# Gating a tile of attention one iteration pair earlier, and moving the splits of y and the gate of the last group in the state-space mixer

## The reference, cut to what matters

```
def mamba2_mixer(h, w_in, ...):
    z, xbc, dt = split(h @ w_in)
    xbc = silu(causal_depthwise_conv(xbc, conv_w, conv_b))
    xs, Bm, Cm = split(xbc)
    y = ssd_chunked(xs, dt, A, Bm, Cm) + d_skip[:, None] * xs
    y = y * silu(z)
    y = rmsnorm(y, gate_norm)
    return y @ w_out

def swa_sink_mixer(h, cos, sin, w_in, sinks, w_out):
    q, k, v, gate = split(h @ w_in)
    ...
    o = einsum(p / denom, vb)
    o = o * silu(gate)
    return o @ w_out
```

## Time and profile before

| what | value |
|---|---|
| median of three executions | 1911.11 us |
| the profiled execution: its own time | 1910.12 us |
| its span, first to last instruction | 1908.2 us |
| mean granted TensorE clock | 0.986 |
| TensorE busy (products) | 1849.4 us, 97% |
| TensorE busy (weight loads) | 1473.4 us, 77% |
| VectorE busy | 1063.2 us, 56% |
| GpSimd busy | 890.2 us, 47% |
| ScalarE busy | 583.2 us, 31% |

### The profile page before, as it was taken

How to read it: one execution, slowest core, us unless ns; L and a number is a source line. 1 busy time by engine, 2 the same in 40 slices (tenths; PEclk the granted TensorE clock), 3 DMA queues, 4 the chain that set the end, 5 groups by cost and what they waited for, 6 DMA issues and landing times.

```text
span 1908.2 us, 25036 instructions
## 1 busy us (share of the span) xinstructions
PE 1849.4 (97%) x9691; PEld 1473.4 (77%) x9691; DVE 1063.2 (56%) x1660; ACT 583.2 (31%) x1035; POOL 890.2 (47%) x902
## 2 busy tenths in 40 slices
PE   7999999899999899999999999999999999999998
PEld 5788888687777577478888888887777788888887
DVE  6888887865778647453333321357778733333212
ACT  3444444512334322142111100136656521111001
POOL 4444445354533155245555555654332455555553
PEclk9999999999999899999999999999999999999999
DMA  8777776568555387848888888986653598888875
GB/s 209 166 151 158 150 160 145 130 160 179 124 123 118 72 187 167 202 97 190 194 194 194 194 182 191 203 188 133 133 127 85 125 200 194 194 191 198 181 173 134
DMA packets 217317, 309.92 MB, mean 162 GB/s; under 512 B 22864, under 2 KB 171504, under 8 KB 217200
## 3 DMA queue, kind: packets, MB, share of 16 engines
q0 software_dynamic: 42912, 148.65, 45.5%
q1 hardware_dynamic: 169872, 154.28, 25.9%
q10 hardware_dynamic: 4416, 5.39, 1.1%
HBM read 153.12 MB, written 2.10 MB: 81 GB/s over the span
## 4 chain that ended last, share of the span: by engine, by line
PE 87%; DVE 7%; ACT 2%; issue 2%; DMA 1%; POOL 1%; ACTq 0%; DVEq 0%; POOLq 0%
PE gp L712 22%; PE gp L714 22%; PE gp L713 22%; PE gp L657 2%; PE gp L684 2%; PE gp L658 2%; PE gp L659 2%; PE mp L978 1%; PE gp L686 1%; PE gp L685 1%; PE mp L1081 1%; DVE m_xs L1847 1%; DMA wl<-stage 1%; PE mp L852 1%; PE mp L944 1%
## 5 line engine op out<-in xcount | busy, mean ns | idle before, releaser
L605 POOL TENSOR_SCALAR wh<-stage 128x1024 fp32r<-128x1024 f32 (+3 forms) x300 | 349.3, 1164 | 900.7 <-PE gp L714 712.4
L712 PE MATMUL gp<-hh,wh 128*128 128x512 f32 x1504 | 602.8, 401 | 2.4 <-DMA wl<-stage 0.9
L713 PE MATMUL gp<-hh,wl 128*128 128x512 f32 x1504 | 587.5, 391 | 0.0
L714 PE MATMUL gp<-hl,wh 128*128 128x512 f32 x1472 | 575.8, 391 | 0.0
L611 POOL TENSOR_SCALAR wl<-stage 128x1024 fp32r<-128x1024 f32 (+2 forms) x298 | 350.8, 1177 | 0.0
L712 PEld LDWEIGHTS gp<-hh,wh 128*128 128x128 f32 x1504 | 283.3, 188 | 73.0 <-issue 12.8
L713 PEld LDWEIGHTS gp<-hh,wl 128*128 128x128 f32 x1504 | 283.7, 189 | 57.1 <-issue 1.5
L714 PEld LDWEIGHTS gp<-hl,wh 128*128 128x128 f32 x1472 | 277.3, 188 | 59.7
L614 POOL DMA_DIRECT2D wl<-stage x298 | 263.9, 886 | 94.7 <-POOL wl L611 86.4
L2262 DVE TENSOR_TENSOR val<-gp,rstd 128x512 f32<-128x512 f32 x44 | 30.4, 692 | 203.9 <-PE gp L714 203.9
L2155 DVE TENSOR_TENSOR xT<-gp,xT 128x512 f32<-128x512 f32 x31 | 21.4, 689 | 194.6 <-PE gp L714 189.7
(11 more groups left out here) (381 smaller groups left out, 2773.2 us busy)
## 6 DMA issues: line engine op xcount, KB each, us to landing
wl<-stage POOLq DMA_DIRECT2D x263, 512.0 KB, 5.2
stage<-ffn_w SPq DMA_DIRECT2D x120, 512.0 KB, 4.5
stage<-ssm_w_in SPq DMA_DIRECT2D x32, 512.0 KB, 5.0
stage<-hg_w_in SPq DMA_DIRECT2D x32, 512.0 KB, 4.5
stage<-ssm_w_in SPq DMA_DIRECT2D x32, 256.0 KB, 3.9
stage<-ssm_w_out SPq DMA_DIRECT2D x16, 512.0 KB, 4.2
stage<-att_w_in SPq DMA_DIRECT2D x14, 512.0 KB, 4.7
stage<-cp_w_in SPq DMA_DIRECT2D x12, 512.0 KB, 5.7
```

The costliest lines, as they stand in the source:

```text
L605: pool.tensor_scalar(wh[:, s, part], stage[:, s, part], 1.0, 1.0, ALU.mult, ALU.mult).then_inc(hi_done, 1)
L712: pe.matmul(bank[:, :], wvh[:, cols], hi(kk), start=start, stop=False)
L713: pe.matmul(bank[:, :], wvl[:, cols], hi(kk), start=False, stop=False)
L714: mm = pe.matmul(bank[:, :], wvh[:, cols], lo(kk), start=False, stop=stop)
```

## The change

In the state-space mixer:

- The first eight tiles of y are split in slot 5 of g = 7 (before: four), tiles 8 and 9 in slot 1 of g = 8, 10 and 11 in slot 2, none in slot 3, and 12 and 13 in slots 4 and 5 as before.
- Ahead of slot 0 of g = 8 TensorE issues six granules of the output projection.
- The two tiles of z of group 7 are written into `raw` and not into `sz`, since `sz` still holds those of group 6. VectorE's order in slots 4 and 5 of g = 7 becomes: take z, conv 3, take z, low halves 0 and 1, line 1909 for both tiles of group 6 (`gate_read`), low halves 2 to 7. The rest of the gate of group 6 (`gate_rest`, lines 1912 to 1917) comes in slot 1 of g = 8, behind low halves 8 and 9. ScalarE's order follows: silu 2, silu of z, high halves 0 and 1, silu 3, silu of z, high halves 2 to 7; the squares of group 6 come in slot 1 of g = 8, behind the decays and the high halves 8 and 9.
- GpSimd waits ahead of the first half of the second unit of `ssm_out` until low half 1 is made.

In attention the first `gate_o` of a head group stands at the end of k = 6.

```diff
-    y_split = [range(0, 4), range(4, 8), range(8, 10), range(10, 12), range(12, 13), range(13, 14)]
+    y_split = [range(0, 8), range(8, 10), range(10, 12), range(0), range(12, 13), range(13, 14)]
...
+        def z_of(g, j):
+            return sz[:, j, :] if g < SG - 1 else raw[:, j, TAPS - 1:]
...
                     else:
                         pool.wait_ge(first_used, before + 1)
+                    if (u, i) == (phases["ssm_out"][0] + 1, 0):
+                        pool.wait_ge(split_done, split0["y"] + 2)
...
+                    if g == SG:
+                        run(gran_out, 6)
                     for slot in range(6):
...
-                        if g == SG and slot:
+                        if g == SG and slot > 1:
                             for k in y_split[slot]:
                                 high_y(k)
...
-                            if slot == 5:
+                            if slot == 5 and g < SG - 1:
                                 silu(g, 3)
...
                                 for h in pair:
                                     decay_between(p, h)
-                            elif slot == 4:
+                                if g == SG and slot == 1:
+                                    for k in y_split[slot]:
+                                        high_y(k)
+                                    gate_square(p - 1, 0)
+                                    gate_square(p - 1, 1)
+                            elif slot == 4 and g != SG - 1:
                                 gate_square(p, 0)
-                            elif slot == 5:
+                            elif slot == 5 and g != SG - 1:
                                 gate_square(p, 1)
...
+                        if g == SG - 1 and slot == 5:
+                            silu(g, 2)
+                            silu_z(g, 0)
+                            high_y(0)
+                            high_y(1)
+                            silu(g, 3)
+                            silu_z(g, 1)
+                            for k in y_split[0][2:]:
+                                high_y(k)
...
                     if j >= 4:
-                        if g:
+                        if g == SG - 1:
+                            dve.wait_ge(conv_done, 4 * g + j - 1)
+                        elif g:
                             dve.wait_ge(yg_ready, 2 * g - 5 + j)
-                        dst = sz[:, j - 4, :]
+                        dst = z_of(g, j - 4)
...
-                            elif slot == 4:
-                                if g == SG - 1:
-                                    conv(g, 3)
+                            elif slot == 4 and g != SG - 1:
                                 gate_y(p, 0)
-                            elif slot == 5:
+                            elif slot == 5 and g != SG - 1:
                                 gate_y(p, 1)
-                        if g < SG and slot >= 4:
+                        if g < SG - 1 and slot >= 4:
                             take(g, slot)
...
                         if g == SG - 1 and slot == 5:
-                            for k in y_split[0]:
+                            take(g, 4)
+                            conv(g, 3)
+                            take(g, 5)
+                            low_y(0)
+                            low_y(1)
+                            gate_read(p, 0)
+                            gate_read(p, 1)
+                            for k in y_split[0][2:]:
                                 low_y(k)
                         if g == SG and slot:
                             for k in y_split[slot]:
                                 low_y(k)
+                            if slot == 1:
+                                gate_rest(p - 1, 0)
+                                gate_rest(p - 1, 1)
...
-                        if h and k == 8:
-                            gate_o(h - 1, 0)
                         if h < KVH:
...
+                        if h and k == 6:
+                            gate_o(h - 1, 0)
```

More of the change, by code:

```diff
@@ L1323, in silu_z @@
                     tile_taken(act, ssm0 + 6 * g + 4 + j)
-                    act.activation(sz[:, j, :], sz[:, j, :], ACT.Silu).then_inc(zsilu_ready, 1)
+                    act.activation(z_of(g, j), z_of(g, j), ACT.Silu).then_inc(zsilu_ready, 1)
                 def copy_B(g):
@@ L1383, in mamba @@
                                     decay_between(p, h)
-                            elif slot == 4:
+                                if g == SG and slot == 1:
[4 more added lines that the diff above has]
+                            elif slot == 4 and g != SG - 1:
                                 gate_square(p, 0)
-                            elif slot == 5:
+                            elif slot == 5 and g != SG - 1:
                                 gate_square(p, 1)
-                        if g < SG:
-                            if g == SG - 1 and slot == 5:
-                                for k in y_split[0]:
-                                    high_y(k)
+                        if g < SG - 1:
                             if slot >= 4:
                                 silu_z(g, slot - 4)
-                            if 2 <= slot < 4:
-                                silu(g, slot - 2)
                             if slot == 4:
                                 silu(g, 2)
+                        if g < SG and 2 <= slot < 4:
+                            silu(g, slot - 2)
+                        if g == SG - 1 and slot == 5:
[7 more added lines that the diff above has]
+                                high_y(k)
                 for k in range(14, 16):
@@ L1899, in recur, with gate_read @@
                     ins.then_inc(h_ready, 1)
-                def gate_y(g, t):
+                def gate_read(g, t):
                     n = 2 * g + t
@@ L1904, in gate_y @@
                     dve.wait_ge(y_ready, n + 1)
-                    dve.wait_ge(zsilu_ready, n + 1)
                     if n >= 2:
@@ L1910, in gate_y, with gate_rest @@
                                              ALU.mult, ALU.add).then_inc(y_read, 1)
+                def gate_rest(g, t):
+                    n = 2 * g + t
+                    v = val[:, t, :]
                     dve.wait_ge(y_read, n + 1)
-                    dve.tensor_tensor(v, v, sz[:, t, :], ALU.mult).then_inc(yg_ready, 1)
+                    dve.wait_ge(zsilu_ready, n + 1)
+                    dve.tensor_tensor(v, v, z_of(g, t), ALU.mult).then_inc(yg_ready, 1)
                     dve.wait_ge(yg_ready, n + 1)
@@ L1922, in gate_y @@
                         ins.then_inc(gate_sq, 1)
+                def gate_y(g, t):
+                    gate_read(g, t)
+                    gate_rest(g, t)
                 def low_y(k):
```

## The result

| | before | changed |
|---|---|---|
| median, us | 1911.4 (1910.83 to 1912.49, 4 runs) | 1898.84 (1896.51 to 1900.0, 4 runs) |
| profiled execution: own time, span | 1910.12, 1908.2 | 1900.0, 1898.2 |
| mean granted clock | 0.986 | 0.989 |

The ratio is 0.9932, with a 95% interval of 0.9915 to 0.9949: faster by 12.6 us in the median, where 14.9 were forecast (1896.2 us, range 1889.0 to 1905.5). A ratio in this text is not the quotient of the two medians beside it, and its interval belongs to the ratio; in the last experiment, where the two differ most, the ratio is 0.9951 and the quotient 0.9937.

A forecast was written before the change was run, and what follows sets the result against it. TensorE, holding 87% of the chain that ended last, was taken as the bound. Attention's -15.5 and the state-space part's +0.6 gave -14.9 on 1910.12, so 1895.2; with 1.0 for the median, 1896.2 us, range 1889 to 1905.5.

The forecast's parts named there:

- part 1a: Before the last group's x turn: removing TensorE's wait (6.2 us) and slow clock (1.9), less 0.1 for semaphores, gains 8.0 us.
- Part 1b: Output products in the last group: TensorE newly waits 3.1 us for half 10 and 2.9 for half 13, plus slow clock.
- The slow clock: TensorE products running below full clock after a long wait: 1.3 us behind each of halves 10 and 13, bounds 0 and 2.6.
- The scan's sum: All state-space edits together: a loss of 0.6 us, bounds a gain of 3.7 and a loss of 4.7.
- Part 2: Attention's first gated tile moved ahead of normalise 3: four rounds gain 15.5 us, bounds 10.4 and 15.8.
- A: Output products cover everything, VectorE is not late at halves 10 and 13: state-space gain 8.0 us, 1887.6 us; chance 0.08.
- B: Attention's waits go but its slow clock stays: 10.4 us gained instead of 15.5, 1901.3 us; chance 0.16.
- C: In attention TensorE waits for the turned tile's copy, not the first gated tile: 1911.7 us, no change; chance 0.05.
- D: VectorE's chain in slots 1 to 4 of the last group, blocked by GpSimd: slower, 1930 us if all blocked; chance 0.04.
- part 1: The state-space edits as a whole: 8.0 us gained at the turn, less later waits and slow clock, a loss of 0.6 us.

The follow-up runs named there:

- the last experiment: The changed kernel run once more with nothing altered: 1899.28 us against 1911.31 for the kernel before, ratio 0.9951.
- the version with the orders mended: Changed kernel with low halves 12 and 13 ahead of the last gated tiles, and group 6's gate rest and squares in slot 3: 1891.69 us, ratio 0.9899.
- the scan alone: The changed kernel with attention's first gate_o back at k = 8, so only the state-space edits remain: 1911.48 us against 1909.66, ratio 1.0006.
- attention alone: The kernel before with only attention's first gate_o moved to k = 6: 1895.93 us, ratio 0.9926.
- the two mended orders: Two kernels: the changed one with low halves 12 and 13 in slot 4 (1895.05 us), and that plus group 6's gate rest in slot 3 (1891.69 us).
- no hold: The changed kernel without GpSimd's wait for low half 1: 1900.56 us, ratio 0.9952.
- the last without granules: The changed kernel without the six granules ahead, and with GpSimd held until low half 7 instead of 1: 1892.54 us, ratio 0.9908.

## Why the prediction was right

- **The bound, and part 1a.** TensorE's list of waits gave both places. The forecast was 0.65 us of waiting at the first half (TensorE free at 357.25, half at 357.9) and a turn at full clock; it was 0.94 and 2.01 us, and the version with the orders mended gained 7.8 against 8.0. Within it one size was off: the prediction counted one GpSimd pair, on halves 2 and 3, and nothing for halves 4 to 7; three pairs fell on the six low halves, and they took 9.96 us. The granules had room for all of it but 0.21 us, so it cost next to nothing here and 1.8 us where the granules were taken away.
- **Part 1b.** The waits for halves 10 and 13 were forecast at 3.1 and 2.9 us and were 3.00 and 2.67. The slow clock, put at 1.3 us on each, was 1.4 (12.34 - 10.97) and 1.6 (6.49 - 4.91) in the first execution, none and 1.6 in the second, and 2.8 and none in the scan alone: a term that went from nothing to 2.8 us, a little beyond the bounds of 0 and 2.6 that the prediction gave it, and no fixed price. The scan's sum was a loss of 0.6 by forecast; it was a loss of 1.1 and a gain of 0.2 in two executions of the whole change, a loss of 0.9 in the profile of the scan alone, and 1.1 us slower by the ratio of its runs (0.0006 of 1910; interval: 1.0 faster to 3.2 slower). Half 10 was late by the chain that the prediction followed, and the two waits repeat within 0.01 us in all three profiles; that the scan's sum came within 0.8 us of the forecast is in part luck, since its slow clock was 3.0, 1.6 and 2.8 us in them. GpSimd's held halves came in time: no wait for a weight stands between 350 and 470.
- **Part 2.** 15.5 us forecast; 14.9 and 14.9 measured in the two executions, 14.8 in attention alone. The rounds were forecast at 6.7, 6.7, 7.0 and 9.6 us and took 6.57, 6.59, 7.10 and 10.11. Only the fourth was off: its turn waited 0.99 us for the normalised probabilities where 0.6 was counted, the tile's own wait was 1.01 against 0.9. The gain of round 4 is 4.0 us, not 4.5. The slow clock in these gains (1.3, 2.6 and 1.2 us) was read from one execution of the kernel before; in the scan alone, with the same waits, it was 2.6 us less. The forecast used it as if it were fixed, and that the measured gain came so close comes in part from measuring against the same profile.
- **The rivals.** A (everything covered) failed where the prediction said, at the place of half 13 in VectorE's order, and at half 10. Its 8.0 us for part 1 come once both orders are mended (7.8); the time measured then was 1891.69 us, a gain of 18.0 where A has 23.5. B is out, since no round shows a clock below 1.00. C is out, since attention alone gives the whole gain. D's place was busy as described, but TensorE's wait there was 3.00 us, no more than the 3.1 of the forecast.
- **The sum.** Scan and attention together gained 13.8 us in the first execution (14.9 - 1.1) and 15.1 in the second (14.9 + 0.2), against 14.9 forecast. The medians give 12.6 and 12.0, and the second ratio (0.9933 to 0.9968) leaves at most 12.8 us. Two things stand between. One is the 2.6 us of slow clock in the attention of the profile before, which another execution doesn't show: without it attention gains 12.3, near the medians; how often either occurs was not counted. The other is the shift of 1.5 us from 465 to 507, where nothing is edited. It is under 0.6 us in five of the profiles here (attention alone, the two mended orders, no hold, and the last without granules) and 1.5 to 1.6 in the other six; both longer and shorter stretches of slow clock stand there, behind the same wait for the gated norm's split. No edit sorts the profiles into these two kinds, so it may be chance as behind half 10, but that was not shown.

## What to carry to other kernels

Look for an operation that an engine issues behind something which comes late anyway: moving one such tile ahead of the normalisation gave the whole gain, with no instruction added. Compare with more than one profile of the kernel before: a gain read from one of them can hold microseconds of slow clock that are not there in the next. When work is pulled ahead to cover a wait, everything that this work needs later must be moved ahead by the same amount; list its inputs by their place in each queue, or the wait comes back some granules later. A stall in a stream of products is paid twice, in the wait and in what the clock does behind it, and the second part changes from execution to execution (0 to 2.8 us behind a wait of 3.0 us here).

## What the runs showed that was not expected

- Six low halves took 9.96 us beside three GpSimd pairs, 7.25 beside two, 3.69 to 3.70 beside none: 1.8 to 2.1 us for each pair, nearly the pair's own length. The prediction had the rows for 1.7 us a pair, but counted one pair where three fell. (Its row of 2.5 us for one operation, at 343.10, is from the scan of group 6 and not of the last group.)
- The granted clock behind the wait of 3.0 us at half 10 was 0.64 in one execution of the changed kernel, 1.00 in another, and 0.50 in the scan alone. Over rounds 1 and 3 of attention, with the same waits of 2.7 and 3.5 us, it was 0.84 and 0.73 in one profile and 1.00 and 0.85 in another. The waits of 1.0 us in attention were followed by none of it (round 4: 1.00).
- Two executions of one kernel differ by up to 5 us in stretches that no edit touches.
